# Scores of the second mixer's attention issued as pairs of heads

## The reference, cut to what matters

```python
def attend_block(args):                      # one block of 128 query tokens
    ...
    s = jnp.einsum('bqhd,bqkhd->bqhk', qb, kg).astype(jnp.float32) * (ATT_HEAD_DIM ** -0.5)
    s = jnp.where(valid[:, :, None, :], s, -jnp.inf)
    p = jax.nn.softmax(s, axis=-1).astype(vg.dtype)
    return jnp.einsum('bqhk,bqkhd->bqhd', p, vg)
...
branches = (pool_branch(u_pool, pool_w, pool_scale),
            dsa_branch(q, k, v, iq, ik, iw, positions),
            memory_branch(mq, mem, w_mem_kv))
merged = jnp.zeros_like(x)
for n in range(N_BRANCH):
    merged = merged + gates[:, :, n] * jnp.einsum('bsc,cd->bsd', branches[n], w_br[n])
```

## Time and profile before

| | us |
|---|---|
| median of 3 runs | 3276.11 (3272.26 to 3283.62) |
| the profiled execution | 3277.92 |
| its span in the trace | 3276.1 |
| the attention stage, layer 0 of the second stack | 1686.0 to 1812.6 of the span |
| the same, layer 1 | 2642.0 to 2768.2 |
| PE busy in the span | 2954.1 (90%) |
| DVE, ACT, POOL busy | 1806.0, 1417.8, 1099.5 |

### The profile page before, as it was taken

The page is one execution under the profiler, slowest core; times in us unless marked ns, Lnnn a source line. Parts: engine busy times, 40 slices in busy tenths (PEclk is TensorE's granted clock), DMA queues, the critical chain, the costliest instruction groups (busy, mean ns, idle before and its releaser), DMA issues.

```text
span 3276.1 us, 45602 instructions
## 1 busy us (share of the span) xinstructions
PE 2954.1 (90%) x13620; PEld 2357.1 (72%) x13620; DVE 1806.0 (55%) x2681; ACT 1417.8 (43%) x2009; POOL 1099.5 (34%) x663
## 2 busy tenths in 40 slices
PE   6888999999979999999999978996699999969993
PEld 4666888876758888866777767885558777758883
DVE  3774543037655431357444258996557543179996
ACT  3525455225354552211345127885111443228882
POOL 2212344543123445444643511111237533601101
PEclk8998999999989999999999988998799999979996
DMA  4212233432122334322321338997213322349993
GB/s 119 59 39 78 81 97 96 165 92 66 33 71 86 100 96 153 112 71 71 94 68 49 105 135 328 411 411 286 61 52 94 84 62 62 122 165 404 411 410 134
DMA packets 373736, 461.51 MB, mean 141 GB/s; under 512 B 33396, under 2 KB 280262, under 8 KB 373512
## 3 DMA queue, kind: packets, MB, share of 16 engines
q1 hardware_dynamic: 353664, 392.05, 35.6%
q0 software_dynamic: 14976, 54.53, 4.3%
q10 hardware_dynamic: 4872, 12.26, 1.1%
HBM read 423.10 MB, written 35.65 MB: 140 GB/s over the span
## 4 chain that ended last, share of the span: by engine, by line
PE 48%; issue 32%; POOL 11%; DVE 4%; DMA 2%; ACT 1%; POOLq 0%; ACTq 0%; SPq 0%; DVEq 0%
POOL unit_lo L407 9%; PE bank L487 7%; PE bank L488 6%; PE bank L2033 4%; PE bank L2170 3%; PE bank L2171 3%; PE bank L2174 3%; PE bank L792 2%; PE bank L2184 2%; PE bank L2188 2%; PE bank L2185 2%; PE bank L2094 1%; PE bank L892 1%; PE bank L893 1%; PE bank L895 1%
## 5 line engine op out<-in xcount | busy, mean ns | idle before, releaser
L407 POOL TENSOR_TENSOR unit_lo<-unit_raw,unit_hi 128x1024 fp32r<-128x1024 f32 (+1 forms) x176 | 422.4, 2402 | 874.5 <-ACT unit_hi L400 874.5
L487 PE MATMUL bank<-xT_hi,unit_hi 128*128 128x512 f32 (+1 forms) x1776 | 700.0, 398 | 13.8 <-ACT cosA L2321 4.2
L488 PE MATMUL bank<-xT_lo,unit_hi 128*128 128x512 f32 (+1 forms) x1776 | 672.6, 382 | 0.0
L487 PEld LDWEIGHTS bank<-xT_hi,unit_hi 128*128 128x128 f32 x1776 | 339.9, 191 | 107.1 <-issue 34.8
L488 PEld LDWEIGHTS bank<-xT_lo,unit_hi 128*128 128x128 f32 x1776 | 340.0, 191 | 66.4 <-issue 7.8
L392 POOL TENSOR_TENSOR unit_lo<-unit_raw,unit_hi 128x1024 fp32r<-128x1024 f32 (+3 forms) x172 | 353.3, 2054 | 14.4
L390 POOL TENSOR_SCALAR unit_hi<-unit_raw 128x1024 fp32r<-128x1024 f32 (+3 forms) x172 | 160.1, 931 | 572.8 <-PE bank L2033 296.5
L400 ACT ACTIVATE unit_hi<-unit_raw 128x1024 fp32r<-128x1024 f32 (+1 forms) x176 | 185.0, 1052 | 382.9 <-PE bank L792 152.7
L472 DVE TENSOR_TENSOR wt_lo<-wt,wt_hi 128x1024 fp32r<-128x1024 f32 x192 | 229.2, 1223 | 33.4 <-ACT wt_hi L467 32.5
L472 DVE TENSOR_TENSOR xT_lo<-wt,xT_hi 128x1024 fp32r<-128x1024 f32 x192 | 234.5, 1223 | 12.5 <-ACT xT_hi L467 2.7
L792 PE MATMUL bank<-xT_hi,unit_lo 128*128 128x512 f32 x976 | 241.0, 389 | 0.0
(11 more groups left out here) (516 smaller groups left out, 6413.3 us busy)
## 6 DMA issues: line engine op xcount, KB each, us to landing
wt<-in_w SPq DMA_DIRECT2D x384, 512.0 KB, 8.7
unit_raw<-in_w_in SPq DMA_DIRECT2D x276, 256.0 KB, 3.1
unit_raw<-in_w_ffn_up SPq DMA_DIRECT2D x176, 256.0 KB, 3.1
unit_raw<-in_w_ffn_down SPq DMA_DIRECT2D x88, 256.0 KB, 3.0
unit_raw<-in_w_out SPq DMA_DIRECT2D x64, 256.0 KB, 2.8
y_rows<-yb POOLq DMA_DIRECT2D x32, 512.0 KB, 7.2
y_rows<-zeros POOLq DMA_DIRECT2D x24, 512.0 KB, 5.2
unit_raw<-in_w_br SPq DMA_DIRECT2D x96, 128.0 KB, 2.2
```

What stands on the lines that cost most here:

```text
L407: pool.eng.tensor_tensor(lo, raw, hi.bitcast(F32), SUB).then_inc(self.split, 1)
L487: pe.matmul(out, wh, xh, start=first, stop=False)
L488: pe.matmul(out, wh, xl, start=False, stop=False)
```

## The change

The loop over 32 heads becomes a loop over 16 pairs, u = 4i + n, the two heads being 2n and 2n + 1 of block i. PE issues both score products next to each other, partitions 0 to 63 into bank 2 and 64 to 127 into bank 3, with one wait before and one signal after both. DVE masks both, reduces both and negates both maxima at once, ACT makes both exponentials. PE's order in an iteration is now: the pair's scores, one piece, the values of pair u - 2, one piece, the transposes of pair u - 1, two pieces. The 72 pieces are the same; ACT looks for due sigmoids at two places of an iteration.

```diff
-    "at_scores": (0, 16, 32),
+    "at_scores": (0, 16, 16),
...
-    "at_max": (0, 16, 32),
+    "at_max": (0, 16, 16),
...
-        A_PIECES = [2] * 35 + [1, 1]
+        A_PIECES = [(1, 1, 2)] * 16 + [(1, 1, 1)] * 2 + [(1, 1, 0)]
+        PAIRS = AH // 2
...
-            for s in range(NT * AH + 5):
-                if s < NT * AH:
-                    i, n = s // AH, s % AH
-                    r, nk = slice(64 * (n % 2), 64 * (n % 2) + 64), (i + 1) * P
-                    if s >= 2:
-                        T.eng.wait_ge(a_sc.sem, a_sc.at(T, s - 1))
-                    pe.matmul(bank[2 + s % 2][:, 0:nk], qk[r, n // 2, i * P:i * P + P], qk[r, 4 + n // 2, 0:nk], start=True, stop=True).then_inc(at_s.sem, at_s.up(T))
-                fill(A_PIECES[s] // 2)
...
+            for u in range(NT * PAIRS + 3):
+                if u < NT * PAIRS:
+                    i, n = u // PAIRS, u % PAIRS
+                    nk = (i + 1) * P
+                    if u:
+                        T.eng.wait_ge(a_sc.sem, a_sc.at(T, 2 * u))
+                    for x, r in enumerate((slice(0, 64), slice(64, P))):
+                        last = pe.matmul(bank[2 + x][:, 0:nk], qk[r, n, i * P:i * P + P], qk[r, 4 + n, 0:nk], start=True, stop=True)
+                    last.then_inc(at_s.sem, at_s.up(T))
+                fill(A_PIECES[u][0])
+                if 0 <= u - 2 < NT * PAIRS:
+                    for k in (2 * u - 4, 2 * u - 3):
+                        i, m = k // AH, k % AH
+                        T.eng.wait_ge(at_te.sem, at_te.at(T, k + 1))
...
+                fill(A_PIECES[u][1])
+                if 0 <= u - 1 < NT * PAIRS:
+                    for k in (2 * u - 2, 2 * u - 1):
+                        T.eng.wait_ge(at_p.sem, at_p.at(T, k + 1))
...
+                fill(A_PIECES[u][2])
...
-                pieces += A_PIECES[s]
+            for u in range(NT * PAIRS + 3):
+                if u < NT * PAIRS:
+                    nk = (u // PAIRS + 1) * P
+                    A.eng.wait_ge(at_mx.sem, at_mx.at(A, u + 1))
+                    for s in (2 * u, 2 * u + 1):
+                        act.activation(sc[s % 4][:, 0:nk], sc[s % 4][:, 0:nk], ACT.Exp, bias=amx[:, s:s + 1],
+                                              accum_out=asum[:, s:s + 1]).then_inc(at_p.sem, at_p.up(A))
+                pieces += A_PIECES[u][0] + A_PIECES[u][1]
                 sigmoids(sigmoids_by(pieces))
...
+                pieces += A_PIECES[u][2]
+                sigmoids(sigmoids_by(pieces))
...
+                    for s in (2 * u, 2 * u + 1):
+                        v.scalar_tensor_tensor(sc[s % 4][:, 0:nk], bank[2 + s % 2][:, 0:nk], HD ** -0.5, mask_of[i], MUL, ADD).then_inc(a_sc.sem, a_sc.up(V))
+                    for s in (2 * u, 2 * u + 1):
+                        V.eng.wait_ge(a_sc.sem, a_sc.at(V, s + 1))
+                        v.tensor_reduce(amx[:, s:s + 1], sc[s % 4][:, 0:nk], AX.X, MAX).then_inc(v_step.sem, v_step.up(V))
...
+                    v.tensor_scalar(amx[:, 2 * u:2 * u + 2], amx[:, 2 * u:2 * u + 2], -1.0, None, MUL).then_inc(at_mx.sem, at_mx.up(V))
+                pieces += sum(A_PIECES[u])
                 products(branches_by(pieces))
```

More of the change, by code:

```diff
@@ new lines, in tensor2 @@
+            for u in range(NT * PAIRS + 3):
[12 more added lines that the diff above has]
+                        T.eng.wait_ge(at_te.sem, at_te.at(T, k + 1))
+                        if m == 0 and i >= 2:
+                            T.eng.wait_ge(a_ol.sem, a_ol.at(T, i - 1))
+                        for x in range(i + 1):
+                            last = pe.matmul(bank[6 + i % 2][:, m * HD:m * HD + HD], apT[k % 2][:, x, :], vv[:, x, m * HD:m * HD + HD],
+                                             start=x == 0, stop=x == i)
+                        last.then_inc(at_o.sem, at_o.up(T))
+                fill(A_PIECES[u][1])
+                if 0 <= u - 1 < NT * PAIRS:
+                    for k in (2 * u - 2, 2 * u - 1):
+                        T.eng.wait_ge(at_p.sem, at_p.at(T, k + 1))
+                        for x in range(k // AH + 1):
+                            last = pe.transpose(bank[4 + k % 2][:, x * P:x * P + P], sc[k % 4][:, x * P:x * P + P], ident)
+                        last.then_inc(at_t.sem, at_t.up(T))
+                fill(A_PIECES[u][2])
+                if u >= 6 and (u - 6) % PAIRS == 0:
+                    i = (u - 6) // PAIRS
@@ L2343, in scalar2 @@
                 sigmoids(sigmoids_by(pieces))
[L2344 to L2349, removed]
-                pieces += A_PIECES[s]
-                sigmoids(sigmoids_by(pieces))
[L2352 to L2360, removed]
+            for u in range(NT * PAIRS + 3):
[6 more added lines that the diff above has]
+                pieces += A_PIECES[u][0] + A_PIECES[u][1]
+                sigmoids(sigmoids_by(pieces))
+                if 0 < u <= NT * PAIRS:
+                    for k in (2 * u - 2, 2 * u - 1):
+                        nk = (k // AH + 1) * P
+                        A.eng.wait_ge(at_t.sem, at_t.at(A, k + 1))
+                        if k >= 2:
+                            A.eng.wait_ge(at_o.sem, at_o.at(A, k - 1))
+                        act.activation(flat(apT[k % 2])[:, 0:nk], bank[4 + k % 2][:, 0:nk], ACT.Copy).then_inc(at_te.sem, at_te.up(A))
+                pieces += A_PIECES[u][2]
+                sigmoids(sigmoids_by(pieces))
+                if u >= 6 and (u - 6) % PAIRS == 0:
+                    i = (u - 6) // PAIRS
                     A.eng.wait_ge(a_ot.sem, a_ot.at(A, i + 1))
@@ L2587, in vector2 @@
                                            over(ars.unsqueeze(2), [P, AH, HD]), MUL).then_inc(a_or.sem, a_or.up(V))
-                if s >= 4 and (s - 4) % AH == AH - 1:
-                    i = (s - 4) // AH
+                if u >= 6 and (u - 6) % PAIRS == 0:
+                    i = (u - 6) // PAIRS
                     V.eng.wait_ge(a_oh.sem, a_oh.at(V, i + 1))
```

40 lines of the change are left out of this document (8 added, 32 removed).

## The result

The changed kernel takes 3248.36 us (3243.65 to 3255.8, 4 runs) beside 3275.69 (3272.26 to 3283.62, 4 runs) for the kernel before: a ratio of 0.9907, with a 95% interval of 0.989 to 0.9923. The time lies in the forecast's range of 3237 to 3258 us and moved the way that was forecast, 3.9 us above the forecast of 3244.5. The profiled execution took 3243.65 us against 3277.92, so 34.3 us less where the sum said 31.6.

What follows compares the result with a forecast made beforehand. PE, busy throughout the stage's widest block, was taken as the bound. Terms of -29.9 (pairs), -2.4 and +0.7 made -31.6 us, taking the median of 3276.1 to 3244.5 us, range 3237 to 3258.

Steps and rivals of the forecast that it cites:

- the sum: Whole kernel: pairs -29.9, gate 10's wait -2.4, gate 16's wait +0.7, together 31.6 us less.
- One score product costs 0.62 to 1.25 us: Score products on PE: 0.21 us per 128 keys plus a constant of 0.40; 29.9 us per layer.
- A pair costs what one product does: Adjacent score products on PE: both halves run at once, 0.62 to 1.25 us per pair, 29.9 us less.
- one after the other: Rival: a pair's products run serially on PE, only one constant saved per pair; 3261.6 us, chance 0.03.
- Passes in program order: Rival: a pair costs three passes on PE, 8.5 us more than forecast; 3253.0 us, chance 0.05.
- this changes nothing. Cost 0.: Score products on PE: standing behind a dense matmul in place of behind values costs 0.
- The wait that goes: PE's wait for gate 10's sigmoid, 1.2 us per layer, disappears with ACT's new order; 2.4 us less.
- The wait that grows: Gate 16's wait for the last d_lo, behind gate 15's product and sum: about 0.35 us per layer, 0.7 more.
- What hides the softmax: PE's other work covers each pair's softmax; tightest at gate 11's sigmoid, which holds by 0.4 us; cost 0.
- sigmoids come late: Rival: each of 16 gates on PE waits 0.5 us for ACT, 8 us lost; 3252.5 us, chance 0.07.
- softmax chain: Rival: softmax becomes the bound, each of 32 pairs waits 1.6 us; 3294.5 us, chance 0.03.
- last sign of being wrong: Stage 15.8 us shorter but span not 31.6 shorter: the next stage waits for something PE does not drive.

Runs made afterwards that it cites:

- e7: Changed kernel with DVE reducing, negating and signalling head by head and ACT waiting for each head; 3253.32 us, one run.
- e10: Changed kernel with DVE taking each row maximum twice, so that a pair's softmax starts later; 3251.5 us, one run.
- e2: Changed kernel with the iteration's first dense piece between the two score products of a pair; 3284.93 us, ratio 1.0021.
- e1: Changed kernel with both products of a pair reading partitions 0 to 63, banks as before; 3269.92 us, ratio 0.9979.
- e6: Changed kernel with the values of pair u - 2 at the end of PE's iteration, directly ahead of the next scores; 3251.91 us, ratio 0.9921.
- e5: Kernel before, with ACT's copy to b_hi one step later, behind gate 10's sigmoid; 3271.72 us, one run.
- e8: Changed kernel with gate 15's product and sum on DVE back behind the last d_lo; 3249.84 us, one run.
- e9: Changed kernel with values just ahead of the next scores while there are scores, and gate 15's product behind the last d_lo; 3250.96 us, ratio 0.991.
- e4: Kernel before, run again unedited; 3280.66 us, ratio 1.0009.
- e3: Changed kernel, run again unedited; 3248.48 us, ratio 0.9914.

## Why the prediction was right, step by step

**PE is the bound of the stage.** Right. Both before and after, the stage is PE's instructions and two or three waits. What e7 did to DVE moved nothing, and what e10 did moved gate 11 and one wait in the tail.

**One score product costs 0.62 to 1.25 us.** This is right for a product behind a dense matmul: with 16 at 15.0 us e2's layer 1 adds up to within 0.2. Too much behind values, see below.

**A pair costs what one product does.** Right. The pair's pieces are 1.06 at 512 keys, and 0.42 to 0.43 behind it as for one, and e1 gives the serial case its price. The rival *one after the other* is out. *Passes in program order* is out too: the second head's first pass has started 0.02 us behind the first head's (the cut above), and the pair at 512 keys takes 1.06, not the 1.5 of three passes. What the Trainium skill says in "TensorE: Matmul & The Clock Gate", Part 2, that matmuls stay in program order, does not hold here if the passes are taken one by one: the second product's first pass doesn't wait for the first product's second. Taken by whole products these traces don't speak against it, as the later of two passes that start together is 7 ns behind. The measurement decides. The draining change of mode of the Trainium skill's "TensorEngine Tiling (Array Packing)", Tiling Modes, fits again: e2's product with dense work on both sides pays the constant that the pair shares.

**"A score product used to stand behind values and now stands behind a dense matmul; ... this changes nothing. Cost 0."** This step failed, though by little. From e6 and e2, a product behind values is 0.05 us cheaper. 28 of the 32 products stood behind values before, which made them 28.5 us per layer and not 29.9; halved, with all of them behind dense matmuls, they are 15.0. The pairs are worth 13.5 per layer, 27.0 in both, not 29.9. The chain pieces in the earlier trace rows could not show it: they begin where the piece ahead is taken to end, and the 0.05 lies in the length of that piece.

**The wait that goes.** Mis-sized on the other side: 1.2 us per layer by the waits, 1.48 by e5. A wait is counted from the modelled end of the matmul ahead, 0.39 us after its start where the next one would have started after 0.23; that is the larger part of the difference, by this working, which no run tests by itself.

**The wait that grows.** 0.35 per layer forecast, 0.26 measured by e8. In the trace of the kernel after, at the end of the stage, the last dense matmuls, DVE's product and sum, then `d_lo`, which answers to the earlier trace rows:

```profile
1788.40 1.07 PE L2034 MATMUL bank<-b_hi,unit_lo 128*128 128x512 f32 x4
...
1789.51 0.70 DVE L2539 TENSOR_TENSOR bank<-sinA,bank 128x512 f32<-128x512 f32 x1 [2.77 <-PE bank L2034]
...
1790.24 0.69 DVE L2541 TENSOR_TENSOR up<-up,bank 128x512 f32<-128x512 f32 x1
...
1790.85 0.68 DVE L2600 TENSOR_TENSOR d_lo<-bank,b_hi 128x512 fp32r<-128x512 f32 x1
...
1791.77 0.47 PE L487 MATMUL bank<-xT_hi,unit_hi 128*128 128x512 f32 x1 [1.86 <-DVE d_lo L2600]
```

`d_lo` starts 2.45 us behind the last dense matmuls' start; before it was 2.17.

**What hides the softmax.** Right, with a margin of 0.3 us at gate 11 where 0.4 was forecast. ACT:

```profile
1727.51 0.69 ACT L2325 ACTIVATE sinA<-bank,pcol 128x512 f32<-128x512 f32 x1
```

and PE, whose next gate starts behind the pair's scores:

```profile
1727.65 0.92 PE L2096 MATMUL bank<-qk 64*128 64x384 f32 x4
1728.49 0.50 PE L487 MATMUL bank<-xT_hi,unit_hi 128*128 128x512 f32 x1
```

1727.51 + 0.69 = 1728.20 against 1728.49. The rival *sigmoids come late* was the nearest one: what e2 and e10 put ahead of this sigmoid PE waited for. The rival *softmax chain* is out: it needed 1 us of wait in every pair, and e10 put 0.6 to 1.4 us on each pair's chain without any transposes waiting.

**The sum.** Per layer -13.5 - 1.48 + 0.26 = -14.7, measured -14.8. For both: 29.4 by the terms, 29.6 measured, 31.6 forecast. That it came out only two off is in part luck: the pairs were taken 2.9 too high and the two waits 0.6 and 0.2 too low, which partly cancel. The prediction's last sign of being wrong, a span that doesn't follow the stages, came true in a small way with the 1.4 us between them. The medians differ by 27.3 us, the ratio's interval allows 25 to 36.

## What to carry to other kernels

Two fp32 products with 64 rows of contraction cost one if they stand directly next to each other, in opposite halves of the partitions and in different banks (one bank for both was not tried); a single dense piece between them takes the whole gain back, and one half for both takes most of it (e1 kept 6.7 us where the changed kernel had 28). Cut a wait's or a product's price not from its own piece of the chain but from the length of the stretch, since starts and modelled ends hide a few hundredths. And where two small operands of DVE are joined into one instruction, look at what POOL does beside it.

## What the runs showed of the hardware that was not expected

**A negation that waits for POOL.** Before, DVE negated one column (128x1); now it negates two (128x2). In the kernel before, 10 of the 64 negations began while POOL was in line 392, and each took its 0.15 us; 8 of them ended before POOL's instruction did. One of them, in the timeline of all engines of the kernel before:

```profile
1707.50 2.39 POOL L392 TENSOR_TENSOR unit_lo<-unit_raw,unit_hi 128x1024 fp32r<-128x1024 f32 x1
...
1708.99 0.15 DVE L2578 TENSOR_SCALAR pcol<-pcol 128x1 f32<-128x1 f32 x1
```

In the kernel after, 8 of 32 did, and each lasted until 0.02 to 0.03 us behind the end of POOL's instruction, the longest 1.50 us. The one in block 1 of layer 1, in the same view of the kernel after:

```profile
1710.79 2.38 POOL L392 TENSOR_TENSOR unit_lo<-unit_raw,unit_hi 128x1024 fp32r<-128x1024 f32 x1
...
1711.70 1.49 DVE L2587 TENSOR_SCALAR pcol<-pcol 128x2 f32<-128x2 f32 x1
```

1710.79 + 2.38 = 1713.17, and 1711.70 + 1.49 = 1713.19. That the second column is what matters is shown by e7, the changed kernel with one column again: 16 of its 64 negations began while POOL was in line 392, none took more than 0.154 us, and one was through 2.1 us before POOL's instruction.

The blocked negations cost nothing here, as no wait of PE hangs on them, but of the 2.2 us per layer in e10 the larger half came from one. The prediction counted the negations as work saved and did not see this. The Trainium skill says it in "SBUF — State Buffer", Who interferes with whom: a DVE instruction in a mode with two ports and a GpSimd instruction share a pair of ports, and the later one is blocked for the whole of the other; and "VectorE: DVE Perf Modes", Mode 2×_2P, gives such a mode to `tensor_scalar` within SBUF, whose operand it splits in halves. These traces agree at line 392, with two columns always blocked and one column never.

**A start that differs by 6 us from one execution to the next.** Ahead of the first stage all kernels run the same program, but the low level of the clock falls at other times. The 6.0 us between the two profiled executions had all come by 334 us of the span. One stretch of the kernel before, from 150 to 162 us:

```profile
150.00:162.00 12.00, 10.40 (x52) 8.16 (x51) 7.95 (x12) 7.33 (x17) 1.10 (x2) 0.86 0.16 44
```

and the same of the kernel after:

```profile
150.00:162.00 12.00, 10.40 (x59) 8.40 (x58) 9.11 (x11) 7.12 (x13) 2.38 (x1) 1.00 0.16 45
```

Between 20 and 50 us the granted clock was 0.66 and 0.72, between 195 and 218 us 0.78 and 0.85. It is not the change's doing: e5, the kernel before but for one step of ACT, has the second pattern,

```profile
150.00:162.00 12.00, 10.40 (x60) 8.38 (x59) 9.08 (x12) 7.72 (x15) 2.37 (x1) 1.00 0.16 44
```

and e6 to e9, which are the changed kernel with edits, have the first; their 1200th matmul starts later than that of e5, by 1.3 us in e6 and by 5.0 to 5.7 in the others. A second choice falls between there and the first stage, a stretch of 1352.3 to 1352.7 us in seven executions and of 1355.5 to 1355.9 in five. The same kernel shows both: from 1000 to 1030 us the clock was 1.00 in the kernel before and 0.94 in e4, which repeats it, and it was 1.00 in the kernel after and 0.94 in e3. What chooses between the patterns stays open. The profiled execution after was of the early kind and the one before of the late, so of the 34.3 us between them 6.0 are chance; without them the changed kernel's would have taken 3249.7, and the sum, 3246.3, was 3.4 too low there.

**A clock that falls only in the variants.** e1 and e2 had 3.4 us of the low level early in the stage: it begins 1.6 us behind the first score product, which itself follows PE's wait of 1.4 us for `bm_lo`. Neither of the two kernels has it there, though the wait and the work ahead are the same. It cost 1.7 us per layer in e1, and more in e2's second layer. The granted clock in the stages of both kernels was 1.00 in all four profiled executions, so neither of the ratios of the changed kernel hangs on it. What brings it on was not tried.
